# A hybrid attention and mixture-of-experts layer: slot tables in bf16, a router that reads rows not yet normalized, and another order of reads in the prologue

## The chip, the cores and the metric

The kernel runs on one core of one Trainium2 chip. Times are device microseconds of one execution; the kernel before took 1896.4 us (median of three runs: 1895.67, 1896.4 and 1913.62). PE is the matrix engine, PEld its weight loads, DVE the vector engine, ACT the scalar engine, POOL GpSimd, SP the engine whose queue issues most transfers.

## The reference

One layer on 1024 tokens of width 1024, all in float32:

```python
mod = silu(c) @ w_ada + b_ada            # 6144 values: sh_a, sc_a, g_a, sh_m, sc_m, g_m
h = rmsnorm(x, g_norm_mix) * (1 + sc_a) + sh_a
x = x + g_a * hybrid_mixer(h, ...)       # three attentions, gated, then y @ w_out
h = rmsnorm(x, g_norm_moe) * (1 + sc_m) + sh_m
scores = sigmoid(h @ w_router)           # 16 experts; the best of 4 groups, its top 2
w = scores of the chosen two, divided by their sum
# tokens sorted by expert into slots of padded blocks: slot_tok, slot_w
x = x + g_m * sum over the slots of slot_w * (silu(h @ w_gate[e]) * (h @ w_up[e])) @ w_down[e]
```

## The kernel before

The program is written by hand for each engine: each has its own instruction list in program order, and semaphores tie them together. Nothing reorders them, so the order of the code is the order on each engine. Tokens go in NT = 8 tiles of P = 128; NK = 8 is the number of 128-wide pieces of the width; a BANK is 512 columns of PSUM.

**Prologue.** The modulation needs `w_ada` in blocks of 1024 x 512 (2048 KB). The first four (scale and shift, two halves each) are wanted before any projection. SP reads the small vectors (`rows`, `pe_rows`), token tiles 0 and 1, then the four blocks, then the first block of `w_in`, then the other token tiles. For each block DVE adds up eight pieces, each times one column of `cond` = silu(c), into one accumulator of 128 x 512 (`ada_row`, L1110 to L1114). PE then sums that over the partitions, four products with a column of ones (`ada_columns`, L1642). DVE makes `mod_a` and `mod_b` out of it (L1098 to L1100), PE turns a token tile (`turn_tokens`, L1658), DVE and ACT scale and shift it into `hT` (L1133, L845), and PE begins the projections (L1709), eight pieces of 512 columns for each tile. POOL computes the rows' 1/rms and clears a strip of `heads` (L682).

**Output projection and router.** For each tile PE multiplies y, split in a high and a low part, with `w_out`, split in the same way: 32 products with the high weights (L1971, L1972), 16 with the low ones (L1978), into two banks. DVE multiplies the two banks by the gate and adds x (L1473, L1475): `x1`. ACT squares and sums it (L1035), POOL makes 1/rms (L776, L777), DVE makes the normalized and modulated row `xn2` (L1487, L1488), PE turns it (L1988), ACT and DVE copy it out of PSUM as `h2T` (L1040, L1480), and PE multiplies it by `w_router` (L1949). PE's list has the products of tile n, the router of tile n-2 and the turning of tile n-1. After the last tile ACT takes the sigmoid (L1043).

**Slot tables.** DVE chooses two experts for each token and ranks them (L1494 to L1557). Then it writes one-hot tables in float32: `hot_b` (block), `hot_t` (block times the number of the token less the place in the block), `hot_p` (place in the block). PE multiplies the places by `hot_t` (L2002) for the token of each slot, and by `hot_b` times the weights (L2006) for the weight of each slot. DVE copies both (L1581, L1583). POOL gathers the first rows (L785, L788), PE turns them (L2013).

**Experts.** Weights are split in high (ACT, L1052) and low parts (DVE, five pieces of 128 x 2048 for each expert, L1589; the sixth on POOL, L801), as the tokens are (ACT L1056, DVE L1595). PE waits for `xs_lo_ok` and `a_ok` and begins (L2023). `a_ok` comes from an empty instruction on DVE's list behind the split (L1612).

## Time and profile before

| | us |
|---|---|
| median of three runs | 1896.4 |
| the profiled execution | 1903.99 |
| its span | 1902.2 |
| PE busy in the span | 1733.8 (91%) |
| DVE busy | 1004.1 (53%) |
| ACT busy | 724.1 (38%) |
| POOL busy | 366.9 (19%) |

An engine's idle time stands behind the instruction that ends it, with what released it. PEclk or the column after the engines is TensorE's granted clock, 1.00 being 2.4 GHz and 0.50 being 1.2 GHz. In the timeline one product on float32 operands shows as two instructions of PE (x8 in a row are four products, when both operands are plain float32); bf16 operands give one.

### The profile page before, as it was taken

What the parts mean: (1) busy time and instruction counts of PE and PEld (TensorE: products, weight loads), DVE (VectorE), ACT (ScalarE), POOL (GpSimd) and SP (SyncE); (2) the same over time, 40 slices, a digit from 0 to 9 for tenths busy, and PEclk for the clock granted to TensorE, in tenths of its full rate; (3) what the DMA queues carried; (4) which work ended last, traced back from release to release, by engine and by line L of the source; (5) the groups of instructions that cost most, each with busy time, mean ns of one, the idle gap of its engine ahead of it and who ended that gap; (6) DMA issues with size and microseconds to landing.
All of it is one profiled execution on the core that took longest, in us unless ns stands there. A gap on an engine that the chain in (4) does not pass through costs nothing.

```text
span 1902.2 us, 23448 instructions
## 1 busy us (share of the span) xinstructions
PE 1733.8 (91%) x8509; PEld 1317.5 (69%) x8509; DVE 1004.1 (53%) x1617; ACT 724.1 (38%) x1251; POOL 366.9 (19%) x315
## 2 busy tenths in 40 slices
PE   1999999789999898999989989999956999999996
PEld 1555564567777676777767766878855888888885
DVE  5554422445444544555545546676554465668485
ACT  0321110334353543435445345432121354456373
POOL 3221140000010101101011011000002352527355
PEclk9999999899999989999999978999966999999998
DMA  9344231122212111211111110654361787889694
GB/s 336 135 165 138 87 85 24 56 67 67 67 55 63 50 34 34 56 45 51 34 51 34 40 50 1 223 207 186 115 221 44 216 294 249 284 265 349 209 371 138
DMA packets 146649, 247.13 MB, mean 130 GB/s; under 512 B 6248, under 2 KB 69808, under 8 KB 145232
## 3 DMA queue, kind: packets, MB, share of 16 engines
q1 hardware_dynamic: 138560, 217.82, 33.8%
q0 software_dynamic: 7984, 27.93, 6.0%
q8 instruction: 64, 1.05, 0.2%
q14 instruction: 41, 0.34, 0.1%
HBM read 210.60 MB, written 36.18 MB: 130 GB/s over the span
## 4 chain that ended last, share of the span: by engine, by line
PE 82%; DVE 9%; issue 3%; DMA 3%; ACT 2%; SPq 0%; POOL 0%; DVEq 0%; ACTq 0%; POOLq 0%
PE psum L1709 10%; PE psum L1808 8%; PE psum L1869 8%; PE psum L2023 4%; PE psum L2024 4%; PE psum L2028 4%; PE psum L1837 4%; PE psum L1729 3%; PE psum L1898 3%; PE psum L1901 2%; PE psum L2066 2%; PE psum L1892 2%; PE psum L2067 2%; PE psum L2071 2%; PE psum L1886 2%
## 5 line engine op out<-in xcount | busy, mean ns | idle before, releaser
L1869 PE MATMUL psum<-kv,arena 128*128 128x64 f32 x1464 | 195.2, 277 | 31.9 <-ACT arena L393 16.5
L755 POOL TENSOR_SCALAR arena<-arena 128x128 f32<-128x128 f32 (+7 forms) x32 | 77.4, 2418 | 755.3 <-ACT arena L982 755.3
L1356 DVE TENSOR_REDUCE negm<-psum 128x1 f32<-128x640 f32 (+7 forms) x128 | 90.4, 707 | 243.0 <-PE psum L1810 238.0
L1869 PEld LDWEIGHTS psum<-kv,arena 128*128 128x128 f32 x1464 | 186.1, 198 | 39.3 <-DVE arena L395 18.2
L1709 PE MATMUL psum<-arena 128*128 128x512 f32 (+2 forms) x512 | 188.7, 522 | 0.0
L959 ACT ACTIVATE arena<-psum,negm 128x640 f32<-128x640 f32 (+7 forms) x128 | 89.4, 699 | 211.9 <-DVE negm L1356 211.7
L2023 PE MATMUL psum<-heads_r,kv_r 128*128 128x512 f32 x384 | 150.8, 393 | 15.2 <-DVE kv_r L1595 15.2
L1837 PE MATMUL psum<-ident,arena 128*128 128x128 f32 x828 | 133.4, 284 | 23.9 <-ACT arena L959 14.4
L1589 DVE TENSOR_TENSOR arena_r<-arena,heads_r 128x2048 fp32r<-128x2048 f32 x64 | 146.7, 2354 | 15.0 <-ACT heads_r L1052 15.0
L1808 PE MATMUL psum<-kv,heads 112*128 112x512 f32 (+7 forms) x384 | 147.5, 489 | 6.3 <-ACT arena L982 5.8
L2024 PE MATMUL psum<-heads_r,kv_r 128*128 128x512 f32 x384 | 150.6, 392 | 0.0
L1709 PEld LDWEIGHTS psum<-arena 128*128 128x128 f32 x512 | 95.9, 192 | 76.6 <-issue 73.7
L1837 PEld LDWEIGHTS psum<-ident,arena 128*128 128x128 f32 x828 | 94.2, 148 | 57.0 <-issue 28.3
L801 POOL TENSOR_TENSOR arena_r<-arena,bc_r 128x2048 fp32r<-128x2048 f32 x16 | 103.0, 6437 | 104.7 <-ACT bc_r L1052 104.6
L1052 ACT ACTIVATE heads_r<-arena 128x2048 fp32r<-128x2048 f32 x64 | 117.2, 1913 | 0.8 <-DMA arena<-in_w_exp_up_dram 0.8
L1808 PEld LDWEIGHTS psum<-kv,heads 112*128 112x128 f32 (+1 forms) x384 | 71.8, 198 | 43.8 <-issue 27.3
L934 ACT ACTIVATE arena_r<-arena 128x512 fp32r<-128x512 f32 x96 | 60.0, 626 | 102.5 <-DMA arena<-in_w_in_dram 76.1
L2028 PE MATMUL psum<-arena_r,kv_r 128*128 128x512 f32 x384 | 95.0, 389 | 0.0
L2023 PEld LDWEIGHTS psum<-heads_r,kv_r 128*128 128x128 f32 x384 | 72.9, 190 | 30.8 <-issue 15.6
L2024 PEld LDWEIGHTS psum<-heads_r,kv_r 128*128 128x128 f32 x384 | 72.9, 190 | 15.2
L2028 PEld LDWEIGHTS psum<-arena_r,kv_r 128*128 128x128 f32 x384 | 72.1, 188 | 15.0
L395 DVE COPY arena<-psum 128x512 f32<-128x512 f32 (+3 forms) x140 | 67.8, 484 | 22.0 <-PE psum L1837 21.5
(400 smaller groups left out, 3358.9 us busy)
## 6 DMA issues: line engine op xcount, KB each, us to landing
arena<-in_w_exp_gate_dram SPq DMA_DIRECT2D x16, 2048.0 KB, 11.8
arena<-in_w_exp_down_dram SPq DMA_DIRECT2D x16, 2048.0 KB, 12.6
arena<-in_w_exp_up_dram SPq DMA_DIRECT2D x16, 2048.0 KB, 13.8
arena<-in_w_in_dram SPq DMA_DIRECT2D x48, 512.0 KB, 4.1
arena<-in_w_ada_dram SPq DMA_DIRECT2D x7, 2048.0 KB, 15.9
z_dram<-arena SPq DMA_DIRECT2D x48, 256.0 KB, 2.3
arena<-z_dram SPq DMA_DIRECT2D x8, 1536.0 KB, 6.7
bc<-in_w_ada_dram SPq DMA_DIRECT2D x4, 2048.0 KB, 7.7
```

The source lines that it names most:

```text
L801: pool.tensor_tensor(ew_lo(e, 2)[:, SLOT // 2:SLOT], w_raw(e, 2)[:, SLOT // 2:SLOT], ew_hi[2][:, SLOT // 2:SLOT].bitcast(F32), ALU.subtrac ...
L959: act.activation(prob[q % 2][:, 0:w], src, ACT.Exp, bias=negm[:, q % 4:q % 4 + 1], accum_out=den[:, u["n"] % 2, col:col + 1]).then_inc(p_o ...
L1052: act.activation(ew_hi[i][:, cs], w_raw(e, i)[:, cs], ACT.Copy).then_inc(w_hi_ok, 1)
L1356: dve.tensor_reduce(m1, score_buf(u)[:, 0:w], AX.X, ALU.max, negate=True).then_inc(max_ok, 1)
L1589: dve.tensor_tensor(ew_lo(e, i)[:, cs], w_raw(e, i)[:, cs], ew_hi[i][:, cs].bitcast(F32), ALU.subtract).then_inc(w_lo_ok, 1)
L1709: mm = pe.matmul(psum[:, 4 + s % 3, 0:w], hT[:, k, n * P:(n + 1) * P], slot(slot_of(L_TOK + ch))[:, k, 0:w], start=(k == 0), stop=(k == NK ...
L1808: mm = pe.matmul(b[:, c0:c1], lhs, keys[:, k0 + c0:k0 + c1], start=True, stop=not masks)
L1837: ins = pe.transpose(bank[:, c * P:(c + 1) * P], src[:, t * P:(t + 1) * P], ident[:, :])
L1869: mm = pe.matmul(psum[:, bank, c * HD:(c + 1) * HD], pt[:, j * P:(j + 1) * P], v, start=(j == 0), stop=(j == u["nb"] - 1))
L2023: pe.matmul(out, xs_hi[:, k, :], w_hi[:, k, :], start=(k == 0), stop=False)
L2024: pe.matmul(out, xs_lo[:, k, :], w_hi[:, k, :], start=False, stop=False)
L2028: mm = pe.matmul(out, xs_hi[:, k, :], w_lo[:, k, :], start=False, stop=(k == NK - 1))
```

## The change

Three parts.

*Prologue.* The small vectors and token tile 0 are read from ACT's queue. SP's queue starts with the blocks of `w_ada`, the fourth in two halves, each with a semaphore of its own; token tile 1 follows. Two of a block's eight pieces (`K_PE`) go to PE, which multiplies the raw block with the column of `cond` into a bank of its own (eight products for each block), and DVE adds up the other six. The two broadcast biases are read later. The constants of `tok` are written before the first block. Token tile 1 is turned into other banks and waits for no one.

*Router.* PE turns `x1` itself, not `xn2`. The modulation scale goes into the router's weights (`wr_a2`), the shift into a row of biases (`rt_bias`, eight more products once), and 1/rms is multiplied in on DVE behind the product. Each half of a tile's output has a count of its own, and its residual runs by halves.

*Tables.* All one-hot tables are bf16. The token's number is split in two exact parts (multiple of 128, rest), the weight in three bf16 parts that DVE adds up. The slot numbers are taken from PSUM before the weights are made, and DVE splits three of the first expert's five pieces before the tokens, two behind them.

(The diff is cut, and its lines are moved twelve columns to the left.)

```diff
+        K_PE = (2, 3)
...
-for r, (src, n) in enumerate(((c, NK), (g_norm_mix, NK), (g_norm_moe, NK))):
-    sp.dma_start(rows[r * NK:(r + 1) * NK, :], src.rearrange("o (k p) -> (o k) p", p=P)).then_inc(small_in, 16)
-sp.dma_start(rows[3 * NK:9 * NK, :], b_ada.rearrange("o (k p) -> (o k) p", p=P)).then_inc(small_in, 16)
-for a, g in enumerate((cmp_pe_k, cmp_pe_v)):
-    sp.dma_start(pe_rows[:, a * HD:(a + 1) * HD], g.rearrange("o l d -> (o l) d")).then_inc(small_in, 16)
-for n in range(2):
-    sp.dma_start(xt[n], x2d[n * P:(n + 1) * P, :]).then_inc(x_in[n], 16)
-for i in ORDER[0:5]:
+for i in ORDER[0:3]:
+place, src = loads[3][0]
+sp.dma_start(place(slot_of(3))[:, 0:4, :], src[:, 0:4, :]).then_inc(ada_half_in, 16)
+sp.dma_start(place(slot_of(3))[:, 4:NK, :], src[:, 4:NK, :]).then_inc(w_in_slot[slot_of(3)], 16)
+sp.dma_start(xt[1], x2d[P:2 * P, :]).then_inc(x_in[1], 16)
+load(ORDER[4])
...
-pool.dma_start(ga_bc[:, :], b_ada[0, 2 * D:3 * D].partition_broadcast(P)).then_inc(gain_in, 16)
-pool.dma_start(gm_bias, b_ada[0, 5 * D:6 * D].partition_broadcast(P)).then_inc(gain_in, 16)
...
 pool.memset(heads[ROW_POS:ROW_SEL, :], 0.0).then_inc(tables, 1)
+pool.wait_ge(tables, 2)
+row_scale(1)
+pool.wait_ge(x_rstd, 2)
+wait_load(pool, L_TOK)
+pool.dma_start(ga_bc[:, :], b_ada[0, 2 * D:3 * D].partition_broadcast(P)).then_inc(bias_in, 16)
+pool.dma_start(gm_bias, b_ada[0, 5 * D:6 * D].partition_broadcast(P)).then_inc(bias_in, 16)
...
+for r, (src, n) in enumerate(vectors):
+    act.dma_start(rows[r * NK:(r + 1) * NK, :], src.rearrange("o (k p) -> (o k) p", p=P)).then_inc(small_in, 16)
+act.dma_start(xt[0], x2d[0:P, :]).then_inc(x_in[0], 16)
...
+    if n:
+        act.wait_ge(xn2T_full, n)
+        act.activation(h2T[:, 4:8, :], psum[:, 5, :].rearrange("p (k t) -> p k t", k=4),
+                       ACT.Copy).then_inc(h2T_act, 1)
-    if n:
-        act.wait_ge(xn2T_full, n)
-        act.activation(h2T[:, 4:8, :], psum[:, 5, :].rearrange("p (k t) -> p k t", k=4),
-                       ACT.Copy).then_inc(h2T_act, 1)
-act.wait_ge(rt_full, NT)
-act.activation(route[0], psum[:, 6, 0:P], ACT.Sigmoid).then_inc(score_ok, 1)
+act.wait_ge(rt_read, NT)
+act.activation(route[0], logits, ACT.Sigmoid).then_inc(score_ok, 1)
...
-for r in range(4):
-    for k in range(NK):
-        ada_row(r, k)
-    if r < 2:
-        row_norm(r)
-dve.wait_ge(turned, 4)
-scale_shift(mod_a, mod_b, psum[:, 7, 0:NK], psum[:, 7, NK:2 * NK], 1, 0, 1).then_inc(mod_ok, 1)
-dve.wait_ge(mod_ok, 1)
-tokens_out_dve(0)
-dve.wait_ge(tables, 2)
-dve.wait_ge(gain_in, 16 * 12)
+for r in range(4):
+    for k in range(NK):
+        if k not in K_PE:
+            ada_row(r, k)
+    if r == 0:
+        row_norm(r)
+    if r == 1:
+        dve.wait_ge(tables, 2)
+        dve.wait_ge(gain_in, 16 * 10)
+        own(dve.tensor_scalar(gain_q8[0:ROW_SEL, :], G_Q[0:ROW_SEL, :], HD ** -0.5, None, ALU.mult))
+        own(dve.tensor_scalar(gain_sq8[:, :], G_SQ, HD ** -0.5, None, ALU.mult))
+dve.wait_ge(ada_direct, 1)
+own(dve.scalar_tensor_tensor(mod_a, psum[:, 6, 0:NK], 1.0, cols[:, 4 * NK:5 * NK], ALU.add, ALU.add))
+own(dve.tensor_tensor(mod_b, psum[:, 6, NK:2 * NK], cols[:, 3 * NK:4 * NK], ALU.add))
+row_norm(1)
+dve.wait_ge(turned, 4)
+own(dve.tensor_tensor(mod[:, 0:2 * NK], mod[:, 0:2 * NK], psum[:, 7, 0:2 * NK], ALU.add))
+dve.tensor_tensor(mod_a, mod_a, cols[:, NK:2 * NK], ALU.mult).then_inc(mod_ok, 1)
+dve.wait_ge(mod_ok, 1)
+tokens_out_dve(0)
...
+def router_logits(n):
+    dve.wait_ge(rt_full, n + 1)
+    dve.scalar_tensor_tensor(logits[:, n * NE:(n + 1) * NE], psum[:, 6 + n % 2, n * NE:(n + 1) * NE], stp[:, 1 + n:2 + n],
+                             rt_bias, ALU.mult, ALU.add).then_inc(rt_read, 1)
+
+def residual(n, h):
+    hs = slice(h * BANK, (h + 1) * BANK)
+    dve.wait_ge(out_full, 2 * n + h + 1)
+    own(dve.tensor_tensor(x1[n % 2][:, hs], psum[:, 2 * (n % 2) + h, :], ga_bc[:, hs], ALU.mult))
+    return dve.tensor_tensor(x1[n % 2][:, hs], x1[n % 2][:, hs], xr[n % 3][:, hs], ALU.add)
...
-        t2 = x1[n % 2].rearrange("p (a d) -> p a d", a=2)
-        own(dve.tensor_tensor(t2, psum[:, 2 * (n % 2):2 * (n % 2) + 2, :],
-                              ga_bc[:, :].rearrange("p (a d) -> p a d", a=2), ALU.mult))
-        dve.tensor_tensor(x1[n % 2], x1[n % 2], xr[n % 2], ALU.add).then_inc(x1_ok, 1)
+        residual(n, 0)
+    if n:
+        m = n - 1
+        dve.wait_ge(xn2T_full, n)
+        dve.tensor_copy(h2T[:, 0:4, :], psum[:, 4, :].rearrange("p (k t) -> p k t", k=4)).then_inc(h2T_dve, 1)
+        dve.wait_ge(x1_rstd, n)
+        dve.wait_ge(x1_ok, n)
+        own(dve.scalar_tensor_tensor(xn2, x1[m % 2], stp[:, 1 + m:2 + m], a2_bc, ALU.mult, ALU.mult))
+        dve.tensor_tensor(xn2, xn2, b2_bc, ALU.add).then_inc(xn2_ok, 1)
+    if n < NT:
+        residual(n, 1).then_inc(x1_ok, 1)
         if n + 2 < NT:
             mixed_lo(n + 2)
-    if n:
-        dve.wait_ge(xn2T_full, n)
-        dve.tensor_copy(h2T[:, 0:4, :], psum[:, 4, :].rearrange("p (k t) -> p k t", k=4)).then_inc(h2T_dve, 1)
-    if n < NT:
-        dve.wait_ge(x1_rstd, n + 1)
-        if n:
-            dve.wait_ge(xn2_out, 16 * n)
-        else:
-            dve.wait_ge(mod_rows_act, 1)
-        own(dve.scalar_tensor_tensor(xn2, x1[n % 2], stp[:, 1:2], a2_bc, ALU.mult, ALU.mult))
-        dve.tensor_tensor(xn2, xn2, b2_bc, ALU.add).then_inc(xn2_ok, 1)
+    if 1 <= n < NT:
+        router_logits(n - 1)
+router_logits(NT - 1)
...
-own(dve.tensor_tensor(hot_t, hot_b, tok_less[:, :].unsqueeze(2).to_broadcast([P, 2 * NT, N_BLK]), ALU.mult))
+own(dve.tensor_tensor(tok_rest[:, :], tok_rest[:, :], pb_f[:, 0, :], ALU.subtract))
+for c, v in enumerate((tile_row, tok_rest)):
+    own(dve.tensor_tensor(hot_t[:, :, c, :], hot_b, v[:, :].unsqueeze(2).to_broadcast([P, 2 * NT, N_BLK]), ALU.mult))
...
+dve.wait_ge(plan_pe, SLOT_FULL)
+own(dve.tensor_scalar(slot_part, psum[:, 6, 0:N_BLK], spare_row[:, 0:1], None, ALU.add))
+dve.tensor_tensor(slot_idx[:, 2:N_BLK + 2], slot_part, psum[:, 6, N_BLK:2 * N_BLK], ALU.add).then_inc(plan_dve, 1)
...
-dve.tensor_tensor(hot_b, hot_b, w12[:, :, :].rearrange("p j n -> p (j n)").unsqueeze(2).to_broadcast([P, 2 * NT, N_BLK]),
-                  ALU.mult).then_inc(hot_w_ok, 1)
-dve.tensor_scalar(slot_idx[:, 2:N_BLK + 2], psum[:, 6, 0:N_BLK], spare_row[:, 0:1], None, ALU.add).then_inc(slot_ok, 1)
-dve.wait_ge(slot_w_full, 1)
-dve.tensor_copy(slot_w[:, 2:N_BLK + 2], psum[:, 4, 0:N_BLK]).then_inc(slot_w_ok, 1)
+own(dve.tensor_copy(w_part[:, :, 0], w16))
+own(dve.tensor_tensor(w_left[:, :], w16, w_part[:, :, 0], ALU.subtract))
+own(dve.tensor_copy(w_part[:, :, 1], w_left[:, :]))
+own(dve.tensor_tensor(w_left[:, :], w_left[:, :], w_part[:, :, 1], ALU.subtract))
+own(dve.tensor_copy(w_part[:, :, 2], w_left[:, :]))
+dve.tensor_tensor(hot_w, hot_b.unsqueeze(2).to_broadcast([P, 2 * NT, 3, N_BLK]),
+                  w_part[:, :, :].unsqueeze(3).to_broadcast([P, 2 * NT, 3, N_BLK]), ALU.mult).then_inc(plan_dve, 1)
...
-expert_weights_lo(0)
+expert_weights_lo(0, range(3))
+dve.wait_ge(plan_pe, SLOT_W_FULL)
+dve.tensor_reduce(slot_w[:, 2:N_BLK + 2], psum[:, 4, 0:3 * N_BLK].rearrange("p (c b) -> p b c", c=3), AX.X,
+                  ALU.add).then_inc(plan_dve, 1)
 expert_tokens_lo(0)
-dve.wait_ge(dest_ok, 1)
+expert_weights_lo(0, range(3, 5))
+dve.wait_ge(plan_dve, DEST)
 n_blk = dve.value_load(plan_i[0:1, 2 * NE:2 * NE + 1], min_val=NE, max_val=N_BLK - 1)
-dve.wait_ge(slot_w_ok, 1)
+dve.wait_ge(plan_dve, SLOT_W)
 dve.nop().then_inc(a_ok, 1)
...
+    if r < 4:
+        if r == 3:
+            pe.wait_ge(ada_half_in, 16)
+        else:
+            wait_load(pe, r)
+        for j in range(4):
+            for k in K_PE:
+                ins = pe.matmul(psum[:, 6, c + j:c + j + 1], ada_slot(slot_of(r))[:, k, j * P:(j + 1) * P],
+                                cond[:, k:k + 1], start=(k == K_PE[0]), stop=(k == K_PE[-1]))
+        if r == 3:
+            ins.then_inc(ada_direct, 1)
...
+pe.wait_ge(cond_ok, 2)
+for r in range(3):
     ada_columns(r)
 turn_tokens(0)
+ada_columns(3)
 turn_tokens(1)
...
-        mm = pe.matmul(psum[:, 6, n * NE:(n + 1) * NE], h2T[:, k, :], wr[:, k, :],
+        mm = pe.matmul(psum[:, 6 + n % 2, n * NE:(n + 1) * NE], h2T[:, k, :], wr_a2[:, k, :],
...
-    if 1 <= n <= NT:
-        if n >= 2:
-            pe.wait_ge(h2T_act, n - 1)
-            pe.wait_ge(h2T_dve, n - 1)
-            router(n - 2)
-        pe.wait_ge(xn2_ok, n)
+        out_high(0)
+        if n == 0:
+            out_high(1)
+            out_low(0)
+            out_low(1)
+            continue
+        out_low(0)
+    if n == 1:
+        pe.wait_ge(x1_ok, 1)
         for k in range(NK):
-            ins = pe.transpose(psum[:, 4 + k // 4, (k % 4) * P:(k % 4 + 1) * P], xn2[:, k * P:(k + 1) * P],
-                               ident[:, :])
-        ins.then_inc(xn2T_full, 1)
-pe.wait_ge(h2T_act, NT)
-pe.wait_ge(h2T_dve, NT)
-router(NT - 1)
+            mm = pe.matmul(psum[:, 7, BANK - NE:BANK], mod_b2[:, k:k + 1].to_broadcast([P, P]), wr[:, k, :],
+                           start=(k == 0), stop=(k == NK - 1))
+        mm.then_inc(rt_bias_full, 1)
+        pe.wait_ge(wr_a2_ok, 1)
+        pe.wait_ge(mod_rows_act, 1)
+    pe.wait_ge(x1_ok, n)
+    for k in range(NK):
+        ins = pe.transpose(psum[:, 4 + k // 4, (k % 4) * P:(k % 4 + 1) * P], x1[(n - 1) % 2][:, k * P:(k + 1) * P],
+                           ident[:, :])
+    ins.then_inc(xn2T_full, 1)
+    if n < NT:
+        out_high(1)
+        out_low(1)
+    pe.wait_ge(h2T_act, n)
+    pe.wait_ge(h2T_dve, n)
+    router(n - 1)
...
-    mm = pe.matmul(psum[:, 6, 0:N_BLK], hot_p[:, a, :], hot_t[:, a, :], start=(a == 0), stop=(a == 2 * NT - 1))
+    mm = pe.matmul(psum[:, 6, 0:2 * N_BLK], hot_p[:, a, :], hot_t[:, a, :, :].rearrange("p c b -> p (c b)"),
-    mm = pe.matmul(psum[:, 4, 0:N_BLK], hot_p[:, a, :], hot_b[:, a, :], start=(a == 0), stop=(a == 2 * NT - 1))
-mm.then_inc(slot_w_full, 1)
+    mm = pe.matmul(psum[:, 4, 0:3 * N_BLK], hot_p[:, a, :], hot_w[:, a, :, :].rearrange("p c b -> p (c b)"),
```

PE's list from its beginning, before. `ones_f` is the column of ones, `bc` holds the token tiles:

```order
L1664 MATMUL psum<-ident,rows 128x72
L1665 MATMUL psum<-ident,pe_rows 128x32
L1642 MATMUL psum<-ones_f,kv 128x1 x16
L1658 MATMUL psum<-ident,bc 128x128 x16
L1709 MATMUL psum<-arena 128x512 x8
```

and now:

```order
L1739 MATMUL psum<-ident,rows 128x32
L1710 MATMUL psum<-cond,arena 128x1 x8
L1716 MATMUL psum<-ones_f,kv 128x1 x4
L1710 MATMUL psum<-cond,arena 128x1 x8
L1716 MATMUL psum<-ones_f,kv 128x1 x4
L1710 MATMUL psum<-cond,arena 128x1 x8
L1716 MATMUL psum<-ones_f,kv 128x1 x4
L1732 MATMUL psum<-ident,bc 128x128 x8
L1710 MATMUL psum<-cond,kv 128x1 x8
L1716 MATMUL psum<-ones_f,kv 128x1 x4
L1732 MATMUL psum<-ident,bc 128x128 x8
L1784 MATMUL psum<-arena 128x512 x8
```

Each block now has eight products on the raw block ahead of its four with the ones, and the turning of tile 0 stands ahead of the last block's products.

PE's list at the end of the output projection, before:

```order
L1978 MATMUL psum<-kv_r,arena_r 128x512 x8
L1949 MATMUL psum<-wr,heads 128x16 x8
L1988 MATMUL psum<-ident,heads 128x128 x8
L1949 MATMUL psum<-wr,heads 128x16 x8
L1988 MATMUL psum<-ident,heads 128x128 x8
L1949 MATMUL psum<-wr,heads 128x16 x8
L1997 MATMUL psum<-chosen,before_b 128x128
```

and now (`rows` is where `wr_a2` lies):

```order
L2058 MATMUL psum<-kv_r,arena_r 128x512 x8
L2026 MATMUL psum<-rows,heads 128x16 x8
L2078 MATMUL psum<-ident,heads 128x128 x8
L2026 MATMUL psum<-rows,heads 128x16 x8
L2090 MATMUL psum<-chosen,before_b 128x128
```

Behind the last product one router and one turning are left where there were three and two less the last tile's share.

DVE's list from the place table `hot_p` to the first expert's tokens, before (`bc` holds the tables, `kv_r` the low part of the tokens):

```order
L1569 TENSOR_TENSOR bc<-swa_bias,pb_f 128x1024 x2
L1572 TENSOR_TENSOR kv<-kv 128x128
L1573 TENSOR_REDUCE w<-kv 128x8
L1572 TENSOR_TENSOR kv<-kv 128x128
L1573 TENSOR_REDUCE w<-kv 128x8
L1574 TENSOR_TENSOR kv<-w 128x8
L1575 RECIPROCAL kv<-kv 128x8
L1577 TENSOR_TENSOR w<-w,kv 128x8 x2
L1578 TENSOR_TENSOR bc<-bc,w 128x512
L1581 TENSOR_SCALAR slot_idx<-psum,spare_row 128x32
L1583 COPY slot_w<-psum 128x32
L1589 TENSOR_TENSOR arena_r<-arena,heads_r 128x2048 x4
```

and now, from the slot numbers on:

```order
L1630 TENSOR_TENSOR slot_idx<-swa_bias,psum 128x32
L1631 TENSOR_TENSOR kv<-w 128x8
L1632 RECIPROCAL kv<-kv 128x8
L1634 TENSOR_TENSOR w<-w,kv 128x8 x2
L1636 CAST w_part<-w 128x16
L1637 TENSOR_TENSOR w_left<-w,w_part 128x16
L1638 CAST w_part<-w_left 128x16
L1639 TENSOR_TENSOR w_left<-w_left,w_part 128x16
L1640 CAST w_part<-w_left 128x16
L1641 TENSOR_TENSOR bc<-bc,w_part 128x1536
L1642 TENSOR_X
```

## Rows read from the trace of the kernel before

**Rows 1.** The page, the chain that ended last by engine.

```profile
PE 82%; DVE 9%; issue 3%; DMA 3%; ACT 2%; SPq 0%; POOL 0%; DVEq 0%; ACTq 0%; POOLq 0%
```

**Rows 2.** Timeline, 0 to 98 us: start, duration, engine, line, idle before.

```profile
11.85 6.92 POOL L682 MEMSET heads<- 32x8192 f32 x1
...
20.23 0.49 DVE L1110 TENSOR_SCALAR kv<-arena,cond 128x512 f32<-128x512 f32 x1 [11.49 <-DMA arena<-in_w_ada_dram]
20.75 4.69 DVE L1112 SCALAR_TENSOR_TENSOR kv<-arena,cond,kv 128x512 f32<-128x512 f32 x6
25.47 0.75 DVE L1114 SCALAR_TENSOR_TENSOR kv<-arena,cond,kv 128x512 f32<-128x512 f32 x1
...
26.25 0.37 SPq L544 DMA_DIRECT2D arena<-in_w_in_dram  x1
...
45.33 1.87 PE L1642 MATMUL psum<-ones_f,kv 128*128 128x1 f32 x8 [4.04 <-DVE kv L1114]
...
47.06 1.95 PE L1658 MATMUL psum<-ident,bc 128*128 128x128 f32 x8
...
49.04 1.50 ACT L845 ACTIVATE arena<-psum,mod 128x128 f32<-128x128 f32 x4 [38.24 <-PE psum L1658]
...
52.42 8.83 PE L1709 MATMUL psum<-arena 128*128 128x512 f32 x16
...
96.62 0.95 PE L1642 MATMUL psum<-ones_f,gab 128*128 128x1 f32 x8
```

**Rows 3.** Transfers issued in 0 to 75 us: KB each, us to landing.

```profile
arena<-in_w_in_dram SPq DMA_DIRECT2D x1, 2048.0 KB, 15.6
```

**Rows 4.** Stretches: busy us of PE, PEld, DVE, ACT, POOL; clock, DMA share, GB/s.

```profile
20.00:57.00 37.00, 15.56 (x55) 12.40 (x56) 29.15 (x64) 4.04 (x10) 0.74 (x2) 1.00 1.04 390
1310.00:1387.00 77.00, 77.00 (x403) 65.89 (x402) 37.05 (x34) 14.54 (x23) 4.45 (x12) 1.00 0.33 119
...
1427.00:1434.00 7.00, 7.00 (x35) 7.00 (x35) 0.33 (x2) 0.00 (x0) 1.30 (x2) 0.50 0.25 77
1455.00:1902.00 447.00, 431.29 (x2008) 352.85 (x2006) 266.01 (x267) 219.36 (x211) 191.35 (x111) 0.99 0.78 255
```

**Rows 5.** Timeline behind the last output tile, engines apart.

```profile
1387.28 1.22 DVE L1473 TENSOR_TENSOR heads<-psum,gab 128x1024 f32<-128x1024 f32 x1 [6.37 <-PE psum L1978]
...
1387.08 1.85 PE L1949 MATMUL psum<-wr,heads 128*128 128x16 f32 x16
...
1391.48 3.60 PE L1949 MATMUL psum<-wr,heads 128*128 128x16 f32 x16 [1.63 <-ACT heads L1040]
...
1389.79 1.06 ACT L1035 ACTIVATE heads<-heads 128x1024 f32<-128x1024 f32 x1 [11.89 <-DVE heads L1475]
...
1401.34 0.28 ACT L1043 ACTIVATE kv<-psum 128x128 f32<-128x128 f32 x1 [3.84 <-PE psum L1949]
```

**Rows 6.** Timeline from the tables to the first expert, engines apart.

```profile
1418.75 2.36 DVE L1569 TENSOR_TENSOR bc<-swa_bias,pb_f 128x1024 f32<-128x1024 f32 x2
...
1427.10 0.25 DVE L1581 TENSOR_SCALAR slot_idx<-psum,spare_row 128x32 uint32<-128x32 f32 x1 [3.26 <-PE psum L2002]
...
1428.60 1.12 POOL L788 DMA_INDIRECT kv<-xn_dram,in_idx  x1 [0.89 <-POOL in_idx L785]
...
1439.40 5.67 POOL L801 TENSOR_TENSOR arena_r<-arena,bc_r 128x2048 fp32r<-128x2048 f32 x1
...
1450.87 0.76 PE L2023 MATMUL psum<-heads_r,kv_r 128*128 128x512 f32 x1 [15.22 <-DVE kv_r L1595]
```

**Rows 7.** Single lines of DVE: ns min/median/max, first and last start.

```profile
L1589 DVE TENSOR_TENSOR arena_r<-arena,heads_r x8: 2279/2284/6579, 1434.0 to 1493.6; 128x2048 fp32r<-128x2048 f32 x8
...
L1321 DVE TENSOR_TENSOR heads_r<-heads,arena_r x8: 1215/1222/2058, 1126.0 to 1190.9; 128x1024 fp32r<-128x1024 f32 x8
...
L1612 DVEq EVENT_SEMAPHORE  x1: 21/21/21, 1437.7 to 1437.7; - x1
```

**Rows 8.** Transfers issued in 1420 to 1452 us: us to landing.

```profile
kv<-xn_dram,in_idx POOLq DMA_INDIRECT x2, 4.9
```

164 lines of the change are left out of this document (96 added, 68 removed).

## The prediction

> **What bounds it now.** I read the chain first: PE carries 82% of it [rows 1], so what shortens PE's work or its three waits counts, and little else. Then the timeline of the three places that the change touches. In the prologue PE's first projection starts at 52.42, and ahead of it stands DVE: it waits for the first block until 20.23, then works through four blocks, eight pieces each [rows 2]. In the output loop PE is busy 77.00 of 77.00 us [rows 4], so nothing can be won inside it; but behind its last product (1387.2, where DVE's wait ends) 14.1 us pass until the sigmoid at 1401.34 [rows 5]. From there to the first expert's product at 1450.87 [rows 6] are 49.5 us in which PE works only on the tables, most of it at clock 0.50 [rows 4]. After that PE is busy 431 of 447 us [rows 4]. Between the places all waits are relative to other engines, so I let a gain at one place reach the end whole.
>
> **Prologue.** One block is 2.10 MB, at 390 GB/s 5.4 us [rows 4]. Before, the block of `w_in` was issued at 26.25 and took 15.6 to land [rows 2, 3]: 41.9. The same data stands ahead of it now, less the two broadcast biases (1.05 MB, 2.7 us), and SP's large reads start some 2.9 us earlier, since eight small issues and tile 0 left its queue. So it lands at 36.3, and counted back: tile 1 at 30.9, the fourth block's halves at 29.6 and 26.9, the others at 24.2, 18.8, 13.4.
> DVE, for a block: 0.5 + 4 x 0.78 + 0.75 = 4.4 instead of 6.0 [rows 2]. It keeps up with the reads. PE, for a block: four products with the ones are 1.87 [rows 2], so the eight on the raw block are 3.7, together 5.6: just over a block's 5.4. PE: raw 13.4 to 17.1; ones, behind DVE's 17.8, to 19.7; second block to 23.4 and 25.3; third to 29.0 and 30.9; turning of tile 0, 1.95, to 32.8; fourth, raw to 36.5, ones to 38.4. Two small DVE operations, 38.8, and `hT` 1.5 later [rows 2]: the first projection at 40.3, where `w_in` has lain since 36.3. That is 12 us less than 52.42. The 16 memsets moved ahead of the first block lie in DVE's wait for it; the small reads on ACT's queue must land a few us before it, for `cond` is made of them.
> Here the clock decides. The four products with the ones took 1.87 here and 0.95 at 96 us [rows 2], so PE ran here at its slow rate, though the stretch from 20 to 57 is recorded at 1.00 [rows 4]. And narrow products seem not to raise it: L2002 and L2006 are 14 us of PE without a gap, and the stretch 1427 to 1434 still shows 0.50 at 7.00 of 7.00 busy [rows 4]. I take the slow rate, and 12.
> The Trainium skill (TensorE: Matmul & The Clock Gate, Part 1) says the opposite: sustained matmul activity releases the throttle. By that the busy prologue would run at 2.4 GHz; this case's 7 us at 0.50 speak against it for products of so few columns.
> Bounds: at the fast rate DVE's 33.1 for the last half and the landing of `w_in` at 36.3 decide: gain 16. Below, POOL: its memset of 6.92 us starts as before near 11.9 [rows 2] and now lies on DVE's first block. Of DVE operations with two SBUF inputs, one beside POOL's L801 took 6.58 instead of 2.28, one beside another POOL operation 2.06 instead of 1.22 [rows 7]. Fully shut out, the first block ends 5 us later and PE follows it: gain 7. No row shows a memset beside such an operation; it reads nothing, so I take it as free.
> The Trainium skill (GPSIMD Engine Reference, 8. Key points) names the sharing of SBUF interfaces with VectorE instructions that have two SBUF inputs; the 6.58 agrees.
>
> **Router.** The loop's products stay: 48 of 512 columns, one router, one turning for each tile. Added is one group of eight narrow products for the biases, as long as a router, 1.7 [rows 5]. DVE has 37.05 busy of 77.00 there [rows 4], and a half residual (0.7 + 0.7) is wanted only after half a tile of products, so no new wait. After the last product, E: PE's router of tile 6 to E+1.8 beside DVE's half residual to E+1.4; turning to E+2.8; copies 0.7; router of tile 7 from E+3.6, 1.85 at the fast or 3.60 at the slow rate [rows 5], to E+5.5 or E+7.2. DVE meanwhile: ACT's square from E+1.5, with its read-out 1.2, POOL 0.8, then `xn2` from E+3.8, two operations of 1024 elements at 1.2: E+6.3 [rows 5, 6]. The last logits stand behind that on DVE's list. Sigmoid at E+6.8 to E+7.7, I take 7.3. Gain 14.1 - 7.3 - 1.7 = 5. Bounds 3 (copies and router at the slow rate, one semaphore more at each step) and 7 (fast rate and the bias group hidden).
>
> **Tables**, in the old clock, from the sigmoid at 1401.34. Up to `hot_b` nothing changes (1417.8). `hot_t` is written twice, 0.7 more; `hot_p` is 2.36 for both halves [rows 6], to 1421.8; the sums of the weights 1.3, 1423.1. PE's 16 products ran 7.04 in float32, now bf16 and one pass each: even at a third of that the last eight are done by 1423.5. Slot numbers, two operations, 1424.1 instead of 1427.35 [rows 6]. POOL issues the gather at 1425.4 instead of 1428.60, 4.9 to land [rows 8]: 1430.3; turning 1.95; ACT's high part to 1433.1. DVE goes on: four small operations 0.8, five for the three parts 1.0, the table of 1536 elements, by 1.18 for 1024 [rows 6], 1.8: 1427.7. Three pieces at 2.2: 1434.4. The sum of slot weights 0.3, the tokens' low part 1.2: 1435.9, PE at 1436.2 instead of 1450.87. Gain 14.7. It is DVE's order that pays: before, DVE stood idle until 1433.9 for PE's second table and then did five pieces, one of them shut out 4.3 us by L801 [rows 7]; now L801 (3.7 behind the turning, 1436.1 to 1441.8) delays only pieces 4 and 5, due at about 1448 for PE. So that cover is thin, 2 us. The new wait on PE is `a_ok` behind the two moved pieces, but its instruction ran at 1437.7, while five operations of DVE were still to run [rows 7]: it does not wait for them.
> Bounds: 10 if L801 starts before the tokens' low part and it has to wait or the bf16 tables cost more, 17 if nothing waits for POOL.
>
> **Sum.** 12 + 5 + 15 = 32 off the profiled 1903.99 (span 1902.2, 1.8 around it): 1872. The median without profile is 7.6 lower, and I take the same 32 off it: 1864.4. Ends: 7 + 3 + 10 = 20 and 16 + 7 + 17 = 40: 1876 and 1856.
>
> **Rivals.**
> *A, PE fast in the prologue.* The products there run at 2.4 GHz since PE is now busy nearly throughout; the blocks' landing bounds. 36 off: 1860. For it: 5.6 busy of 5.4. Against: rows 4. Chance 0.15.
> *B, POOL shuts DVE out.* Memset on the first block (-5), and L801 on the tokens' low part or on pieces that PE waits for (-5). 22 off: 1874. For it: 6.58. Chance 0.17.
> *C, the experts' start is gated anyway* by `a_ok` or by the two moved pieces: PE at 1436 + 2 x 2.2 + 4.3 + 1 = 1446. Tables gain 5, in all 22: 1874. For it: the place of the instruction behind them. Against: rows 7. Chance 0.08.
> *D, slower: DVE's list in the output loop.* For each tile now stand in a row: half residual 1.4, wait for ACT's square and high part 2.1, low part 1.2, logits 0.2: 4.9 us, all behind the last product. If PE waits for it, because the next half is due earlier than I think, it is paid in eight tiles: 39 us against 32 gained, 1903. It decides from the point at which that row is longer than half a tile's products, 24 x 0.227 = 5.4. Against: 37 of 77 busy. Chance 0.04.
> The forecast itself has 0.56. What small effects of the clock do between the places (a short fall costs a few us) is in none of these.
>
> **Range.** From A to B and C, and two to five us more for the clock: 1851 to 1879. One per cent is 19 us, about what a measurement of this kernel can tell from no change, so faster by over 1% ends at 1877.4: forecast, A, B and C but for a tail, 0.88. Within 1%: 0.08. Slower: 0.04.
>
> **What would show it.** The first projection near 40 (36 if A, 45 if B), products on the raw block at 0.46 us each; the sigmoid 7 us behind the last product with `w_out`; slot numbers 23 behind the sigmoid; the first expert's product 35 behind it; PE still 77 of 77 in the loop. It is wrong if PE waits in the loop, if the first expert starts only behind five pieces, or if the small reads land later than the first block.

## The result and the profile after

| | before | changed |
|---|---|---|
| profiled execution | 1903.99 us, span 1902.2 | 1873.43 us, span 1871.7 |
| median of 8 runs each | 1901.12 us (1895.67 to 1914.41) | 1877.06 us (1873.43 to 1889.39) |

The ratio is 0.9871, with a 95% interval of 0.9832 to 0.9909: faster by 1.3%. That it is more than one per cent is likely and not settled, since the interval ends at 0.9909. In medians that is 24.1 us, in the two profiled executions 30.5. The difference between these two numbers is the first thing to explain, and a table by stages does it. Each stage ends at an instruction that both traces have (for the changed kernel the new line numbers): the first projection, the first turning of the modulation rows (before L1956, now L2033), the first half or whole residual of the last tile (L1473, L1511: PE's last product with `w_out` has ended), the sigmoid, the first expert's product, the end.

| stage | before | changed | difference | the change's own, forecast |
|---|---|---|---|---|
| to the first projection | 52.42 | 47.48 | -4.9 | -12 |
| to the turning of the modulation rows | 1229.80 | 1222.30 | -7.5 | 0 |
| output loop, to its last product | 105.06 | 110.14 | +5.1 | +1.7 |
| to the sigmoid | 14.06 | 6.26 | -7.8 | -6.8 |
| to the first expert's product | 49.53 | 34.00 | -15.5 | -14.7 |
| experts | 451.33 | 451.52 | +0.2 | 0 |

The second stage, 1230 us of attention, is not touched, and yet 7.5 us shorter. Nearly all of it arises in one place. These are the answers for one stretch of each trace that holds the same work (200 and 201 products; columns: length, busy us of PE, of the weight loads, of DVE, ACT and POOL, then granted clock, DMA share, GB/s), of before first, then of the changed kernel:

```profile
1085.00:1135.00 50.00, 43.64 (x200) 30.60 (x199) 23.05 (x30) 20.85 (x35) 8.26 (x2) 0.80 0.17 53
```

```profile
1079.00:1122.00 43.00, 36.23 (x201) 26.03 (x200) 22.29 (x29) 21.25 (x35) 8.26 (x2) 0.96 0.18 62
```

The clock was granted at 0.80 in the one and 0.96 in the other, and 7 us lie between the lengths. Such falls come and go: in the twelve traces of this study, in which this stage is always the same work, it took 1222 to 1235 us. The two with the old prologue and router (1229.8 and 1234.5) lie among the ten with the new ones (1222.3 to 1235.4). So the 7.5 us are taken as chance of the two executions shown. What the change itself gives is the sum of the other rows, 4.9 + 2.7 + 15.5 = 23.1 us, and the medians say 24.1. The remaining 1.0 is not explained.

The chain that ended last is no help here: on the page after it is followed back through the experts only and breaks off, so that its shares do not compare with [rows 1]:

```profile
PE 22%; DVE 1%; issue 0%; DMA 0%; ACT 0%; POOL 0%; DVEq 0%; ACTq 0%; POOLq 0%
```

The prologue of the changed kernel, from its timeline (start us, duration us, engine, line, output and input; in brackets the idle time before it and what ended it), which answers to [rows 2]:

```profile
10.46 0.36 PE L1738 MATMUL psum<-ident,rows 72*128 72x72 f32 x1 [10.46 <-DMA rows<-in_cmp_pe_v_dram]
...
13.84 3.57 PE L1710 MATMUL psum<-cond,arena 128*128 128x1 f32 x16 [2.78 <-DVE cond L1116]
...
13.85 1.94 DVE L1169 MEMSET arena<- 128x1 f32 x16
...
15.35 6.92 POOL L690 MEMSET heads<- 32x8192 f32 x1
...
15.82 6.73 DVE L1136 TENSOR_SCALAR kv<-arena,cond 128x512 f32<-128x512 f32 x1
...
22.58 3.11 DVE L1140 SCALAR_TENSOR_TENSOR kv<-arena,cond,kv 128x512 f32<-128x512 f32 x4
...
26.54 1.87 PE L1716 MATMUL psum<-ones_f,kv 128*128 128x1 f32 x8 [9.13 <-DVE kv L1142]
...
31.68 1.85 PE L1716 MATMUL psum<-ones_f,kv 128*128 128x1 f32 x8
...
47.48 8.51 PE L1784 MATMUL psum<-arena 128*128 128x512 f32 x16 [0.30 <-DVE arena L1162]
...
36.83 0.63 POOL L695 DMA_DIRECT2D gab<-in_b_ada_dram  x1 [4.16 <-DMA arena<-in_w_in_dram]
```

Read it beside the forecast. The eight narrow products on the raw block (x16 in the trace, where each float32 product is two records) take 3.57 us (forecast 3.7: the slow rate), from ones to ones PE takes 5.14 (26.54 to 31.68; forecast 5.6), and `w_in` has landed at 36.8, for POOL's issue behind it starts there (forecast 36.3). But `cond` is ready only at 13.8. Then DVE writes the constants of `tok` (sixteen small memsets, 1.94 us) and begins the first piece at 15.82, and this one operation of 512 elements takes 6.73 us that takes 0.48 elsewhere. It ends at 22.55, and POOL's memset at 22.27. All that follows hangs on it. The order of these times matters: without the sixteen memsets ahead of it the piece could have begun at 13.9, 1.5 us before POOL's memset. This is an estimate from the times above; no run took them away.

The output loop: first PE's products from the first one with `w_out` to about 2 us behind the last, grouped by line (busy us, mean ns), of before, then of the changed kernel; then, from the changed kernel's timeline, what stands behind the last product, answering to [rows 5].

```profile
L1971 PE MATMUL psum<-arena_r 128*128 128x512 f32 x128 | 50.5, 395 | 0.0
...
L1949 PE MATMUL psum<-wr,heads 128*128 128x16 f32 x96 | 11.1, 257 | 0.0
...
L1988 PE MATMUL psum<-ident,heads 128*128 128x128 f32 x50 | 6.8, 277 | 0.0
```

```profile
L2050 PE MATMUL psum<-arena_r 128*128 128x512 f32 x128 | 51.3, 401 | 0.0
...
L2026 PE MATMUL psum<-rows,heads 128*128 128x16 f32 x112 | 13.0, 257 | 0.0
...
L2078 PE MATMUL psum<-ident,heads 128*128 128x128 f32 x58 | 7.7, 274 | 0.0
...
L2071 PE MATMUL psum<-wr,mod 128*128 128x16 f32 x16 | 1.9, 257 | 0.0
```

```profile
1379.92 0.69 DVE L1511 TENSOR_TENSOR heads<-psum,gab 128x512 f32<-128x512 f32 x1 [1.79 <-PE psum L2058]
...
1383.32 2.10 PE L2026 MATMUL psum<-rows,heads 128*128 128x16 f32 x16 [0.83 <-ACT heads L1054]
...
1386.18 0.31 ACT L1064 ACTIVATE kv<-heads 128x128 f32<-128x128 f32 x1 [3.06 <-DVE heads L1505]
```

The sigmoid stands 6.3 us behind the last product instead of 14.1. The counts say why the loop grew by more than the bias row. Each stretch also holds the first router behind the last product (16 records) and two records of the turning behind that. Without them the loop has 96 records of router products instead of 80, which is one tile's router (13.0 - 11.1 = 1.9 us), and 56 of turning instead of 48, one tile's (0.9 us). Before, these two stood behind the last product: three routers and two turnings stood there, and two routers and one turning are left, as PE's list under the change shows (its sentence says one router). They were moved, not saved.

The tables and the first expert, answering to [rows 6]:

```profile
1408.20 0.19 DVE L1630 TENSOR_TENSOR slot_idx<-swa_bias,psum 128x32 uint32<-128x32 f32 x1
...
1409.63 1.12 POOL L803 DMA_INDIRECT kv<-xn_dram,in_idx  x1 [0.89 <-POOL in_idx L800]
...
1411.89 6.69 DVE L1648 TENSOR_TENSOR arena_r<-arena,heads_r 128x2048 fp32r<-128x2048 f32 x3
...
1412.02 1.46 PE L2100 MATMUL psum<-bc 128*128 128x96 bf16 x16 [4.65 <-DVE bc L1641]
...
1418.66 1.28 DVE L1654 TENSOR_TENSOR kv_r<-psum,kv_r 128x512 fp32r<-128x512 f32 x2
...
1420.18 0.77 PE L2118 MATMUL psum<-heads_r,kv_r 128*128 128x512 f32 x1 [3.12 <-DVE kv_r L1654]
...
1420.44 6.12 POOL L816 TENSOR_TENSOR arena_r<-arena,bc_r 128x2048 fp32r<-128x2048 f32 x1
...
1422.06 6.65 DVE L1648 TENSOR_TENSOR arena_r<-arena,bc_r 128x2048 fp32r<-128x2048 f32 x1
```

The slot numbers stand 22.0 us behind the sigmoid, and DVE works on three pieces of the first expert's weights (1411.89) while PE multiplies the second table (1412.02, 1.46 us for 16 products instead of 7.0) and the gather lands. The fifth piece is shut out by POOL's piece for 4.4 us (6.65 instead of 2.28) and delays nobody: it is done at 1428.7.

### The profile page after: what moved, and what is told of

It reads as the page before. It is cut to its first block and busy times, and to the rows that moved or that the text cites. A ratio compares the mean times of both kernels' runs of the same rounds, so it can differ in the third digit from the quotient of the medians.

```text
span 1871.7 us, 23577 instructions
## 1 busy us (share of the span) xinstructions
PE 1726.8 (92%) x8557; PEld 1312.3 (70%) x8557; DVE 1011.2 (54%) x1643; ACT 725.6 (39%) x1251; POOL 367.1 (20%) x316
## 3 DMA queue, kind: packets, MB, share of 16 engines
q8 instruction: 64, 1.05, 0.2%
## 5 line engine op out<-in xcount | busy, mean ns | idle before, releaser
L1912 PE MATMUL psum<-ident,arena 128*128 128x128 f32 x828 | 131.7, 281 | 22.9 <-ACT arena L980 13.4
L1648 DVE TENSOR_TENSOR arena_r<-arena,heads_r 128x2048 fp32r<-128x2048 f32 x64 | 142.4, 2286 | 15.0 <-ACT heads_r L1073 15.0
L816 POOL TENSOR_TENSOR arena_r<-arena,bc_r 128x2048 fp32r<-128x2048 f32 x16 | 102.9, 6433 | 105.1 <-ACT bc_r L1073 105.1
L2118 PEld LDWEIGHTS psum<-heads_r,kv_r 128*128 128x128 f32 x384 | 73.1, 190 | 18.8 <-DVEq L1675 3.5
## 6 DMA issues: line engine op xcount, KB each, us to landing
arena<-in_w_exp_up_dram SPq DMA_DIRECT2D x16, 2048.0 KB, 13.4
```

The source lines that it names most:

```text
L816: pool.tensor_tensor(ew_lo(e, 2)[:, SLOT // 2:SLOT], w_raw(e, 2)[:, SLOT // 2:SLOT], ew_hi[2][:, SLOT // 2:SLOT].bitcast(F32), ALU.subtrac ...
L1648: dve.tensor_tensor(ew_lo(e, i)[:, cs], w_raw(e, i)[:, cs], ew_hi[i][:, cs].bitcast(F32), ALU.subtract).then_inc(w_lo_ok, 1)
L1912: ins = pe.transpose(bank[:, c * P:(c + 1) * P], src[:, t * P:(t + 1) * P], ident[:, :])
L2118: pe.matmul(out, xs_hi[:, k, :], w_hi[:, k, :], start=(k == 0), stop=False)
```

## The experiments

Eight edited kernels ran once each, and the changed kernel and one of the eight were then timed with six runs each. A span carries the chance of the clock, so single runs are compared between the trace's own places.

### The memset moved out of DVE's way

```diff
             pool.memset(half[:, :], -0.5).then_inc(tables, 1)
+            pool.wait_ge(tables, 1)
+            pool.memset(heads[ROW_POS:ROW_SEL, :], 0.0).then_inc(tables, 1)
+            pool.wait_ge(tables, 2)
...
             row_scale(0)
             pool.wait_ge(x_rstd, 1)
-            pool.memset(heads[ROW_POS:ROW_SEL, :], 0.0).then_inc(tables, 1)
-            pool.wait_ge(tables, 2)
```

> The changed kernel, with POOL's memset of 32 rows of heads (6.9 us) moved to the head of POOL's list, ahead of its small DMA issues, so that it runs from 2.4 to 9.4 us, while DVE is still idle. Theory (the memset shuts DVE out of SBUF while it runs, so DVE's first piece took 6.73 us instead of 0.48): DVE's first piece takes 0.5 us and is done near 16.4, the first products with the ones start near 20.4 instead of 26.5, and PE then works without a gap at its slow rate, so that the first projection starts near 42 instead of 47.5. Rival (DVE's first piece waited inside for something else, the landing of the first block or the reads themselves, which use SBUF at the same time): it still takes over 4 us, and the first projection stays within 1.5 us of 47.5. Second rival (the later blocks have not landed when DVE wants them): the first piece is short, but the first projection starts at 44 to 46. The rest of the kernel is unchanged, so the span is shorter by the same amount, within what the granted clock does (some 5 us).

Timeline of that kernel (memset; DVE's first piece; the first products with the ones; the first projection):

```profile
2.54 6.92 POOL L672 MEMSET heads<- 32x8192 f32 x1
...
8.43 0.35 PE L1739 MATMUL psum<-ident,rows 72*128 72x72 f32 x1 [8.43 <-DMA rows<-in_cmp_pe_v_dram]
...
13.79 0.62 DVE L1137 TENSOR_SCALAR kv<-arena,cond 128x512 f32<-128x512 f32 x1
...
18.40 1.86 PE L1717 MATMUL psum<-ones_f,kv 128*128 128x1 f32 x8 [3.02 <-DVE kv L1143]
...
39.33 8.24 PE L1785 MATMUL psum<-arena 128*128 128x512 f32 x16 [0.30 <-DVE arena L1163]
```

The first piece takes 0.62 us, and the first projection starts at 39.33, 8.1 us earlier than in the changed kernel and a microsecond earlier than the forecast had it. 6.1 us of that are the piece. The other 2.0 came unasked: the small reads landed at 8.43 instead of 10.46. That is more than chance: they landed at 8.43 to 9.15 in the three kernels with the memset first and the small reads on ACT's queue, and at 9.81 to 10.79 in the six with the memset in its old place. In this kernel POOL issues its own small reads only from 9.77 on, behind the memset; that they had stood in the way is argued from this, no run took them away alone. DVE's sixteen memsets are on the path here: `cond` is ready at 11.8, PE starts on the block at once, and DVE's first piece starts at 13.79. Neither rival holds: the blocks had landed when they were wanted.

The span of this run was 1877.1, longer than the changed kernel's 1871.7, for the stage of attention took 1233.6 us instead of 1222.3, and the output loop 111.8 instead of 110.1 (so also in s2_small_on_sp; in the other seven runs with the same loop it is 110.1). Whether the gain is kept needs timed runs, below.

### The small reads back on SP's queue

```diff
+            for r, (src, n) in enumerate(vectors):
+                sp.dma_start(rows[r * NK:(r + 1) * NK, :], ...).then_inc(small_in, 16)
...
             for i in ORDER[0:3]:
                 load(i)
...
-            for r, (src, n) in enumerate(vectors):
-                act.dma_start(rows[r * NK:(r + 1) * NK, :], ...).then_inc(small_in, 16)
...
```

> As s1_memset_first, and the six small reads (the vectors, the biases' rows, the position rows) stand again on SP's queue ahead of the blocks instead of on ACT's beside them. Theory (on ACT's queue the small reads share the DMA engines with three large blocks and land at 10.4 instead of 5.1 us, so that cond is ready at 13.8 instead of 8.7): cond is ready near 9, but each block lands some 2.5 us later, the first near 15.5, so the first projection moves by no more than 1.5 us either way against s1_memset_first. Rival (cond is what the prologue waits for, the blocks had landed long before): the first projection starts 4 to 5 us earlier than in s1_memset_first, near 37 to 38.

```profile
5.33 0.35 PE L1739 MATMUL psum<-ident,rows 72*128 72x72 f32 x1 [5.33 <-DMA rows<-in_cmp_pe_v_dram]
...
8.04 1.45 DVE L1115 TENSOR_SCALAR cond<-cond 128x8 f32<-128x8 f32 x1 [1.62 <-ACT cond L856]
...
11.42 3.54 PE L1711 MATMUL psum<-cond,arena 128*128 128x1 f32 x16 [5.50 <-DMA arena<-in_w_ada_dram]
...
24.74 3.57 PE L1711 MATMUL psum<-cond,arena 128*128 128x1 f32 x16 [0.22 <-DMA arena<-in_w_ada_dram]
```

The small reads land at 5.33, `cond` is ready at 9.9, but PE now waits for the blocks: the first lands at 11.42 and the third at 24.74, where the idle time before the product ends with the transfer. The first projection stands at 39.97, 0.6 later than with the reads on ACT's queue. Only the landing of the first block was mis-sized in the expectation (11.4, not 15.5). So with the memset gone the two orders are worth the same: what `cond` wins the blocks lose. At the second block DVE's wait ends with its transfer at 18.2. The landings 11.4, 18.2 and 24.7 are the only direct sight of the blocks' pace: 6.8 and 6.5 us here, where the forecast counted 5.4. One more thing shows here: POOL's memset runs from 2.54 to 9.46, and DVE's operation on eight elements (8.04) takes 1.45 us instead of 0.17 and ends at 9.49.

### The memset twice

```diff
+            one(pool.memset(heads[ROW_POS:ROW_SEL, :], 0.0))
             pool.memset(heads[ROW_POS:ROW_SEL, :], 0.0).then_inc(tables, 1)
```

> The changed kernel with POOL's memset made twice in a row in its place, so that POOL writes from 15.4 to about 29.3 us. Theory (a running POOL memset shuts out DVE's operations on SBUF): DVE gets only what lies in the gap between the two memsets, its first block is done near 33 instead of 26.5, and the first projection starts 6 to 7 us later, near 54. Rival (DVE was held for another cause, which happened to end at 22.5): DVE goes on at 22.5 as before, its operations take their usual 0.5 and 0.78 us beside the second memset, and the first projection stays near 47.5. Middle (one operation is held up, others go through): operations of two inputs run at their usual time while those of one input are held, and the delay is 0 to 3 us.

```profile
14.92 6.92 POOL L690 MEMSET heads<- 32x8192 f32 x1
...
21.90 7.09 POOL L691 MEMSET heads<- 32x8192 f32 x1
...
15.56 6.57 DVE L1137 TENSOR_SCALAR kv<-arena,cond 128x512 f32<-128x512 f32 x1
...
22.16 3.11 DVE L1141 SCALAR_TENSOR_TENSOR kv<-arena,cond,kv 128x512 f32<-128x512 f32 x4
...
25.98 3.56 DVE L1158 TENSOR_SCALAR bc<-bc,stp 128x1024 f32<-128x1024 f32 x1
```

This run tells the mechanism. The one-input product with `cond` (TENSOR_SCALAR, 15.56) is held until the first memset ends. The four operations of two inputs behind it (SCALAR_TENSOR_TENSOR, 22.16) run wholly beside the second memset, which started at 21.90, and take 3.11 us as always. The next one-input operation (25.98, 1024 elements) takes 3.56 us instead of 0.75: it ends at 29.5, and the second memset ends at 28.99. So the memset does not shut DVE out; it holds its one-input operations from SBUF to SBUF, and lets those of two inputs pass. In s2_small_on_sp the two copies out of PSUM (5.96 and 6.18) also ran beside the memset at their usual 0.19 and 0.23 us. The first projection stands at 49.73, 2.3 us later than in the changed kernel, and the theory of the expectation (54) is wrong, its middle case right.

The operations that were held are DVE's fast ones: the two sizes of the one-input operation, 0.48 us for 512 elements and 0.75 for 1024, differ by 0.53 ns for each further element, and those of two inputs, 0.69 for 512 and 1.23 for 1024, by 1.05. The Trainium skill (VectorE: DVE Perf Modes, Mode 2×_2P) says that an operation on one SBUF tensor can take both of DVE's read and both of its write ports and double its rate, and (GPSIMD Engine Reference, 8. Key points) that POOL shares its interfaces with DVE's instructions of this mode or of two SBUF inputs. What they say of this mode agrees with the 6.57 and 3.56 us. What the second says of two SBUF inputs is not seen beside a memset: the 3.11 us stayed.

### The first piece as an operation of two inputs

If that is so, the memset can stay where it is. DVE sets the first block's sum to zero while it is idle, and the first piece is added to it:

```diff
+            own(dve.memset(ada_acc(0), 0.0))
             dve.wait_ge(rowsT, 1)
...
-                    own(dve.tensor_scalar(acc, w, cond[:, k:k + 1], None, ALU.mult))
+                    if r == 0:
+                        own(dve.scalar_tensor_tensor(acc, w, cond[:, k:k + 1], acc, ALU.mult, ALU.add))
+                    else:
+                        own(dve.tensor_scalar(acc, w, cond[:, k:k + 1], None, ALU.mult))
```

> The changed kernel, POOL's memset left where it is (beside DVE's first block), but the first block's first piece written as an operation of two tensor inputs (the piece times cond plus a sum that DVE sets to zero while it is idle) instead of the one-input product that took 6.73 us. Theory, from the run with two memsets, where the operations of two inputs ran at 0.78 us beside the second memset and the one-input ones were held until its end: nothing holds DVE any more, the first piece takes 0.75 to 0.8 us, the first block is done near 21 instead of 26.5, and the first projection starts near 41.5 to 42.5 instead of 47.5. Rival (whatever DVE does first behind the memset's start is held until its end, and what follows is let through): the first piece again takes over 6 us and the first projection stays at 47 to 48.

```profile
14.61 6.92 POOL L690 MEMSET heads<- 32x8192 f32 x1
...
15.24 0.75 DVE L1138 SCALAR_TENSOR_TENSOR kv<-arena,cond,kv 128x512 f32<-128x512 f32 x1
...
19.84 2.23 DVE L1161 TENSOR_SCALAR bc<-bc,stp 128x1024 f32<-128x1024 f32 x1
...
42.33 9.31 PE L1788 MATMUL psum<-arena 128*128 128x512 f32 x16 [0.36 <-DVE arena L1166]
```

Beside the same memset the first piece takes 0.75 us, and the first projection starts at 42.33 instead of 47.48. What is still held is the one-input scaling of tile 0 (19.84, 2.23 us instead of 0.75), until the memset ends at 21.53. Of the 5.15 us some 0.65 are the small reads, which landed at 9.81 here instead of 10.46. One operation written in its slower form wins the other 4.5: 6.0 at the piece, less 1.5 at the scaling. The rival is answered too: the first operation beside the memset was not held.

### All pieces on DVE

As the first experiment (memset first), with `K_PE = ()`, PE's products on the raw block and the two reads of their sums left out:

```diff
-        K_PE = (2, 3)
+        K_PE = ()
...
-            own(dve.scalar_tensor_tensor(mod_a, psum[:, 6, 0:NK], 1.0, cols[:, 4 * NK:5 * NK], ALU.add, ALU.add))
-            own(dve.tensor_tensor(mod_b, psum[:, 6, NK:2 * NK], cols[:, 3 * NK:4 * NK], ALU.add))
+            own(dve.tensor_scalar(mod_a, cols[:, 4 * NK:5 * NK], 1.0, None, ALU.add))
+            own(dve.tensor_copy(mod_b, cols[:, 3 * NK:4 * NK]))
```

> As s1_memset_first, but all eight pieces of each modulation block are done by DVE and none by PE. Theory (PE at its slow rate is now as long for a block, 3.5 and 1.85, as DVE was alone, so that sharing gives little once nothing shuts DVE out): DVE takes 6.0 us for a block, its four blocks end near 41 instead of 36.5, PE's ones follow with 1.9, the first projection starts within 2 us of s1_memset_first, near 43.5. Rival (sharing is what the prologue gained by, as the forecast had it): the first projection is 4 to 6 us later than in s1_memset_first, near 47.

```profile
20.83 1.84 PE L1705 MATMUL psum<-ones_f,kv 128*128 128x1 f32 x8 [11.09 <-DVE kv L1143]
...
27.31 1.87 PE L1705 MATMUL psum<-ones_f,kv 128*128 128x1 f32 x8 [4.64 <-DVE kv L1143]
...
43.48 8.46 PE L1773 MATMUL psum<-arena 128*128 128x512 f32 x16 [0.30 <-DVE arena L1163]
```

The first projection starts at 43.48, where the expectation of the theory had 43.5; but s1_memset_first came out at 39.33 and not at 42, so the difference is 4.2 us. Of these, 0.7 are the small reads, which landed at 9.15 here and at 8.43 there; counted from their landing, the first projection stands at 34.3 and 30.9. So sharing the pieces is worth 3.4 us. The theory (within 2 us) fails, and the rival (4 to 6) has the right cause and is a little high. From block to block DVE alone takes 5.9 to 6.5 us (6.5 from 20.83 to 27.31), and shared it is 5.1.

### DVE's list and the bf16 tables, each alone

The changed kernel with the old list:

```diff
-            expert_weights_lo(0, range(3))
             dve.wait_ge(plan_pe, SLOT_W_FULL)
             dve.tensor_reduce(slot_w[:, 2:N_BLK + 2], ...)
+            expert_weights_lo(0)
             expert_tokens_lo(0)
-            expert_weights_lo(0, range(3, 5))
```

> The changed kernel (bf16 slot tables) with DVE's old list behind the tables: wait for the second table and sum the slot weights, then all five pieces of the first expert's low part, then the tokens' low part. Theory (it is DVE's order that pays, not the cheaper products): the pieces start near 27.5 us behind the sigmoid, one of them is shut out by POOL's piece, the first expert's product stands 43 to 46 us behind the sigmoid instead of 34.0 (before: 49.5). Rival (the cheaper bf16 products pay, the order is worth little): 34 to 38 us behind the sigmoid.

The kernel before with the new list:

```diff
-            dve.wait_ge(slot_w_full, 1)
-            dve.tensor_copy(slot_w[:, 2:N_BLK + 2], psum[:, 4, 0:N_BLK]).then_inc(slot_w_ok, 1)
...
-            expert_weights_lo(0)
+            expert_weights_lo(0, range(3))
+            dve.wait_ge(slot_w_full, 1)
+            dve.tensor_copy(slot_w[:, 2:N_BLK + 2], psum[:, 4, 0:N_BLK]).then_inc(slot_w_ok, 1)
             expert_tokens_lo(0)
+            expert_weights_lo(0, range(3, 5))
```

> The kernel before (float32 slot tables, 7 us for each table on PE), with DVE's new list only: three pieces of the first expert's low part, then the slot weights, then the tokens' low part, then the last two pieces. Theory (the order pays): DVE does the three pieces while PE works on the second table and the gather lands, the first expert's product stands 36.5 to 38.5 us behind the sigmoid instead of 49.5, so the order alone gives 11 to 13 of the 15.5 us. Rival (the products bound, DVE's list is not on the path): 45 to 49 us behind the sigmoid. Third (the bf16 tables and the order are both needed): 40 to 44.

The us from the sigmoid to the first expert's product:

| | old list | new list |
|---|---|---|
| float32 tables | 49.5 | 39.1 |
| bf16 tables | 44.4 | 34.0 |

The list gives 10.4 us in either row, the tables 5.1 or 5.2 in either column; they add up. The order gives two thirds of the 15.5 us, and the bf16 tables one third. The first expectation is met (44.4 in 43 to 46). The second is missed by a little: 39.1 lies in none of its three ranges, nearest to the theory's 36.5 to 38.5, and 10.4 is less than its 11 to 13. The trace with the old list shows why, and that with float32 tables and the new list shows what POOL pays for it (first fence: bf16 tables, old list; second: float32 tables, new list):

```profile
1424.08 8.89 DVE L1648 TENSOR_TENSOR arena_r<-arena,heads_r 128x2048 fp32r<-128x2048 f32 x4
...
1431.65 5.67 POOL L816 TENSOR_TENSOR arena_r<-arena,bc_r 128x2048 fp32r<-128x2048 f32 x1
...
1432.88 6.58 DVE L1648 TENSOR_TENSOR arena_r<-arena,bc_r 128x2048 fp32r<-128x2048 f32 x1
```

```profile
1431.99 6.69 DVE L1587 TENSOR_TENSOR arena_r<-arena,heads_r 128x2048 fp32r<-128x2048 f32 x3
...
1432.25 2.06 POOL L785 COPY in_idx<-slot_idx 128x1 uint32<-128x1 uint32 x1 [35.69 <-DVE slot_idx L1581]
...
1435.20 2.25 POOL L788 DMA_INDIRECT kv<-xn_dram,in_idx  x1 [0.89 <-POOL in_idx L785]
...
1440.95 1.97 PE L2014 MATMUL psum<-ident,kv 128*128 128x128 f32 x8 [2.34 <-DMA kv<-xn_dram,in_idx]
```

In the old list the five pieces stand ahead of the tokens' low part, and the last of them is held by POOL's piece (6.58). In the second kernel the roles are exchanged: DVE's pieces start at once behind the slot numbers, and POOL's copy of one index column, 0.18 us elsewhere, takes 2.06 beside them, and its gather's issue 2.25 instead of 1.12. The tokens are turned at 1440.95. In the changed kernel POOL's copy and issue fall into the time in which DVE makes the weight table from small operations, and are not held (0.19 and 1.12 us). The forecast had not seen this.

### Without the bias row

The router's logits lack the modulation's shift here, so other experts are chosen; the 1836.2 us of its span, with 414 us of experts instead of 451, say nothing about the change.

```diff
-                    for k in range(NK):
-                        mm = pe.matmul(psum[:, 7, BANK - NE:BANK], mod_b2[:, k:k + 1].to_broadcast([P, P]), wr[:, k, :], ...)
-                    mm.then_inc(rt_bias_full, 1)
...
-                    dve.wait_ge(rt_bias_full, 1)
-                    own(dve.tensor_copy(rt_bias, psum[:, 7, BANK - NE:BANK]))
+                    own(dve.memset(rt_bias, 0.0))
```

> The changed kernel without PE's group of eight narrow products that makes the router's bias row; the row is set to zero instead, so the router's logits lack the modulation's shift. Measured between the trace's own places: from the turning of the modulation rows to the last product with w_out PE takes 110.1 us in the changed kernel and 105.1 before. Theory (of these 5.1 us the bias group is 1.9, and the rest is one router, 1.85, and one turning, 1.0, of a tile that used to stand behind the last product, plus some switches between long and short products): 108.2 without the group, and 6.3 from there to the sigmoid as now. Rival (PE waits for DVE's longer list in the loop): the loop stays over 109.5, since the wait takes the group's place. Second rival (the bias group is all that was added): 105 to 106.

The output loop took 108.40 us instead of 110.14. So the group costs 1.7 us, and 3.3 us of growth remain. By the rows above they are the router and the turning that were moved in, 2.8 together, and some 1.0 by which the long products with the high weights grew (L2050 51.3 instead of 50.5 us, L2051 50.0 instead of 49.8). PE now goes from narrow products to long ones twice in each tile instead of once; that this is why they grew is not shown. The sum is 0.5 too much, and durations of neighbouring products overlap a little. PE waited 0.8 us in all, for ACT, and that behind the last tile. There is no wait of rival D's kind. The tail took 7.3 us instead of 6.3 in this run: its last router ran at the slow rate (3.56 us instead of 2.10).

### Timed: the changed kernel and the one with the memset first

> The changed kernel once more, timed beside t_memset_first on the same chip: 23 to 26 us less than the kernel before in the median (ratio near 0.987), since its gains by stage are 4.9 (prologue), 2.7 (router) and 15.5 (tables), 23.1 together, and the rest of the 30.5 between the two profiled executions is the granted clock.

> The same kernel as s1_memset_first, timed. Theory (a gain ahead of the first projection reaches the end whole, and the late projections of the one look, 11 us of lower clock between 380 and 1160 us, were chance): 8 us less than t_changed in the median, a ratio near 0.983 to the kernel before. Rival (the clock is granted as the work is done, so that what PE gains early is given back as falls of the clock later): within 2 us of t_changed, near 0.987.

| | median | lowest to highest | ratio to before | 95% interval |
|---|---|---|---|---|
| kernel before, 11 runs | 1904.96 us | 1896.69 to 1909.57 | | |
| changed, 6 runs | 1878.92 us | 1875.17 to 1886.47 | 0.9876 | 0.9848 to 0.9905 |
| memset first, 6 runs | 1867.96 us | 1866.67 to 1879.17 | 0.9820 | 0.9791 to 0.9849 |

The changed kernel is 26.0 us below the kernel before, at the upper end of the expected 23 to 26. The two intervals only touch, and the medians differ by 11 us where 8 were expected. In the two profiled executions of these runs the first projection stands at 47.14 and 39.34, the attention took 1226.2 and 1226.9 us, the output loop 110.15 and 110.14, and the spans are 1875.5 and 1868.3. The gain of 7.8 us reaches the end but for 0.6, and the rival, by which the clock takes it back, falls. This kernel, the changed one with two lines moved and a wait added, is 1.8% below the kernel before, the fastest of those timed more than once. The kernel with the first piece as an operation of two inputs took 1869.95 us in its one run, as long as the profiled one here (1870.0).

## Why the prediction was right, and where it was not

The predicted time was 1864.4 us with a range of 1851 to 1879; measured were 1877.1. The direction and the range hold, the time is 12.7 us off, and two errors in one direction make it up. The gains were 23.1 us by stage instead of 32, 8.9 less (7.9 by the medians). And the 32 were taken off the 1896.4 us that three runs had as their median; with eight runs it is 1901.1, 4.7 more. That the range holds owes something to luck: the time lies 1.9 us inside its end, and 0.3 inside the prediction's own bound for over one per cent, 1877.4.

**Prologue, forecast 12, measured 4.9.** The step that failed is "it reads nothing, so I take it as free", on POOL's memset. Its price was 6.1 us of DVE and, with the small reads that landed 2.0 later than in s1_memset_first, 8.1 us at the first projection. The prediction had a price of this size as its bound and as rival B (fully shut out the block ends 5 us later, first projection 45), and left it out because the memset has no input. The memset lay in DVE's wait for the first block before the change (it ended at 18.8 and DVE started at 20.2 [rows 2]); the earlier block exposed it, and it also began later, at 15.35 instead of the forecast 11.9. In [rows 7] only operations with two SBUF inputs were held, so the price was looked for there, and the runs showed the opposite kind held by a memset: for the products of two inputs "free" was right, for the one product of one input it was wrong. A second step failed with it: "The 16 memsets moved ahead of the first block lie in DVE's wait for it". They ran from 13.85 to 15.79, behind `cond`, when the block had landed (PE was working on it from 13.84), and so, by these times, they pushed the first piece into POOL's memset.

The rest of this step stood. With POOL's memset out of the way the first projection is at 39.3, forecast 40.3. That it is so near is in part two errors that cancel: the first block was there by 11.8 and not at 13.4, and the sixteen memsets cost DVE 1.9 us behind it. The products on the raw block took 3.57 for 3.7, at the slow rate, against rival A; `w_in` landed at 36.8 for 36.3. The block's pace of 5.6 on PE was 5.1. The trace of the changed kernel shows no landing of a block, since nothing waits for one; with the small reads on SP the first came at 11.4 and the third at 24.7. SP's first large read was issued at 0.81 instead of 4.17, 3.4 us earlier where the sum had 2.9.

**The late small reads.** The prediction said that they "must land a few us before it", the first block, and named it as what would make it wrong; but it gave no number. They landed at 10.46, where the trace of before has 5.11, since on ACT's queue they run beside three blocks instead of ahead of them. With POOL's memset out of the way this costs nothing (s2_small_on_sp): earlier small reads are later blocks. In the changed kernel it had another effect. ACT squares tile 0 only behind its part of `cond` (at 13.19 us, before the change at 8.41), and POOL's 1/rms and its memset follow that. So the late small reads also moved the memset onto the first block. What the small reads on SP's queue would give with the memset in its old place no run shows.

**Router, forecast 5, measured 2.7.** The tail was right (7.8 us less for 6.8), the bias row was right (1.7 in the experiment, 1.7 assumed, though the router it was read from is 1.85 in [rows 5]). What failed is "The loop's products stay: 48 of 512 columns, one router, one turning for each tile". They stay in number for the whole kernel; but the sum was made from the last product on, and one router and one turning changed sides of it. They shortened the tail, for which the forecast counted them, and lengthened the loop by 2.8 us, for which it did not. "PE still 77 of 77 in the loop" came true (107.00 of 107.00 us busy from 1272 on) and could not show this.

**Tables, forecast 14.7, measured 15.5.** Slot numbers 22.0 behind the sigmoid (22.8), first expert 34.0 (34.9). "It is DVE's order that pays" is two thirds of it by the four combinations: the order gives 10.4 us, and the cheaper tables 5.1. Rival C (a wait for the two moved pieces) falls: PE started at 1420.18, and the fifth piece ended at 1428.7. L801, now L816, held only this fifth piece, as said.

**Rival B** gives 1874 and came nearest to the median, 1877.1; its first half, the memset, is what happened (though to an operation of one input, where it argued from those of two), its second, POOL's piece on the tokens' low part, is not. The time of the profiled execution, 1873.43, is near B for another reason: 7.5 us of it are the clock's.

## What to carry to other kernels

When an edit brings data earlier, look at what the receiving engine's wait used to hide: an operation of another engine that lay in this wait for nothing may now lie on the path, and here DVE's one-input operations were those that stood still beside POOL's memset, while its two-input ones stood still beside POOL's operation of two inputs. Where work is moved across the point at which a sum begins, count it on both sides. And stage by stage between instructions that both traces share, a change of one per cent can be read from two traces, while their two totals can differ by 7 us of granted clock alone.

## What the runs showed of the hardware

- A POOL memset of 32 rows by 8192 float32 (6.92 us) holds DVE's one-input operations from SBUF to SBUF until it ends (512 elements: 0.48 became 6.73 and 6.57 us; 1024: 0.75 became 3.56 and 2.23; 8: 0.17 became 1.45). It does not hold those of two SBUF inputs (3.11 us for four, with and without it) nor DVE's copies out of PSUM (0.19 and 0.23 us, with and without it).
- DVE's operations of two inputs and POOL's operations that read SBUF hold each other both ways. DVE's piece took 6.65 us instead of 2.28 beside POOL's piece. POOL's copy of 128x1 took 2.06 instead of 0.18 beside DVE's pieces, and its issue of the gather 2.25 instead of 1.12.
- The products of the prologue took the time of the slow rate all through: 1.85 to 1.87 us for four products with the ones (0.95 at 96 us before [rows 2]), and 1.95 for the turning of a tile (1.07 behind the output loop). Yet PE worked almost without a gap from 26.5 to 45 us (18.46 of 19.00 us busy from 26 to 45), and the record of the granted clock has 1.00 there.
- The same attention stage took 1222 to 1235 us in twelve executions, with the granted clock of the whole run between 0.955 and 0.967.
